# Merge-gate tiles of the second hybrid layer and value tiles of the spatial mixer: two matmuls a block with halves added by VectorE, in place of three

## The reference

```python
def hybrid_layer(x, y, ...):            # called for layer 0 and layer 1
    hx = rms_norm(x, norm_w) * (1.0 + scale_x) + shift_x
    rq, rk, rv, rg, nq, nk, nv, ng, gq, gk, gv, gg, mg = split_cols(hx @ w_in)
...
def merge_branches(ret_o, na_o, gqa_o, gate_logits, w_ret_o, w_na_o, w_gqa_o, w_out):
    g_ret, g_na, g_gqa = jnp.split(jax.nn.sigmoid(gate_logits), 3, axis=-1)
    m = g_ret * (ret_o @ w_ret_o) + g_na * (na_o @ w_na_o) + g_gqa * (gqa_o @ w_gqa_o)
    return m @ w_out
...
def spatial_gating_mixer(x, w_in, v_norm, w_s, b_s, w_out):
    u, v = jnp.split(jax.nn.gelu(x @ w_in), 2, axis=-1)
    v = rms_norm_2(v, v_norm)
```

## Time and profile before

| | |
|---|---|
| median of 3 runs | 1982.38 us (1981.38 to 1985.36) |
| the profiled execution | 1981.85 us, of which the span in the trace is 1980.1 us |
| TensorE busy | 1952.4 us, 99% of the span, 13237 matmuls |
| VectorE busy | 1217.8 us, 62% |
| ScalarE busy | 891.7 us, 45% |
| mean granted clock of TensorE | 0.998 |

### The profile page before, as it was taken

How to read it: one execution, slowest core, us unless ns; L and a number is a source line. 1 busy time by engine, 2 the same in 40 slices (tenths; PEclk the granted TensorE clock), 3 DMA queues, 4 the chain that set the end, 5 groups by cost and what they waited for, 6 DMA issues and landing times. The chain is left out here.

```text
span 1980.1 us, 35364 instructions
## 1 busy us (share of the span) xinstructions
PE 1952.4 (99%) x13237; PEld 1705.6 (86%) x13237; DVE 1217.8 (62%) x1965; ACT 891.7 (45%) x1422; POOL 218.0 (11%) x230
## 2 busy tenths in 40 slices
PE   8999999999999999999999999999999999999998
PEld 6777887777787788998998999989998999999997
DVE  6554443355443655546567777887678677677675
ACT  5444232244432544335554445764445444554443
POOL 1000100111122101211111000000001000201000
PEclk9999999999999999999999999999999999999999
DMA  8221443411234323343355554445555555445553
GB/s 324 78 73 66 147 145 129 142 62 57 82 104 159 105 94 106 108 139 118 128 171 182 188 182 167 155 158 190 181 185 198 181 186 185 160 150 181 181 187 109
DMA packets 79429, 289.23 MB, mean 146 GB/s; under 512 B 8912, under 2 KB 9168, under 8 KB 79312
## 3 DMA queue, kind: packets, MB, share of 16 engines
q1 hardware_dynamic: 77616, 281.61, 42.2%
q0 software_dynamic: 1120, 4.72, 0.8%
q10 hardware_dynamic: 576, 1.24, 0.2%
HBM read 286.49 MB, written 1.05 MB: 145 GB/s over the span
## 5 line engine op out<-in xcount | busy, mean ns | idle before, releaser
L1947 DVE TENSOR_TENSOR w_lo<-raw,w_hi 128x1024 fp32r<-128x1024 f32 x484 | 597.8, 1240 | 306.5 <-ACT w_hi L1643 305.7
L1643 ACT ACTIVATE w_hi<-raw 128x1024 fp32r<-128x1024 f32 x484 | 507.5, 1055 | 405.5 <-PE bank L2562 249.6
L2568 PE MATMUL bank<-h,w_hi 128*128 128x512 f32 x1376 | 491.1, 399 | 1.3 <-DVE h L2069 0.8
L2560 PE MATMUL bank<-h,w_hi 128*128 128x512 f32 (+1 forms) x1344 | 473.2, 352 | 3.6 <-issue 1.7
L2561 PE MATMUL bank<-h,w_hi 128*128 128x512 f32 (+1 forms) x1344 | 452.9, 337 | 0.0
L2562 PE MATMUL bank<-h,w_lo 128*128 128x512 f32 (+1 forms) x1344 | 452.4, 337 | 0.0
L2570 PE MATMUL bank<-h,w_lo 128*128 128x256 f32 x1376 | 386.3, 281 | 0.0
L2568 PEld LDWEIGHTS bank<-h,w_hi 128*128 128x128 f32 x1376 | 258.7, 188 | 62.0 <-DVE h L2069 1.4
L2560 PEld LDWEIGHTS bank<-h,w_hi 128*128 128x128 f32 x1344 | 254.5, 189 | 54.1 <-issue 28.2
L2562 PEld LDWEIGHTS bank<-h,w_lo 128*128 128x128 f32 x1344 | 254.6, 189 | 27.9
L2561 PEld LDWEIGHTS bank<-h,w_hi 128*128 128x128 f32 x1344 | 255.1, 190 | 24.2 <-issue 1.9
(11 more groups left out here) (257 smaller groups left out, 2366.1 us busy)
## 6 DMA issues: line engine op xcount, KB each, us to landing
raw<-in_weights SPq DMA_DIRECT2D x516, 512.0 KB, 3.3
early<-in_first SPq DMA_DIRECT2D x10, 512.0 KB, 13.4
bias<-in_rpb POOLq DMA_DIRECT2D x8, 384.0 KB, 3.4
early_o<-in_first SPq DMA_DIRECT2D x4, 512.0 KB, 16.3
x<-in_tokens SPq DMA_DIRECT2D x2, 512.0 KB, 6.0
x<-in_tokens ACTq DMA_DIRECT2D x2, 512.0 KB, 8.6
work<-in_first SPq DMA_DIRECT2D x2, 512.0 KB, 16.6
out<-cols_out SPq DMA_DIRECT2D x4, 256.0 KB, 2.5
```

The costliest lines, as they stand in the source:

```text
L1643: nc.scalar.activation(w_hi[:, n % SPLIT, :], raw[:, t % RAW, :], ACT.Copy).then_inc(hi_ready, 1)
L1947: dve.tensor_tensor(w_lo[:, t % RAW, :], raw[:, t % RAW, :], w_hi[:, SPLIT_NO[t] % SPLIT, :].bitcast(F32), ALU.subtract).then_inc(lo_ready, 1)
L2560: nc.tensor.matmul(dst, w_hi[:, SPLIT_NO[t] % SPLIT, at], hi, start=start, stop=False, skip_group_check=shared)
L2568: nc.tensor.matmul(bank[:, :], w_hi[:, SPLIT_NO[t] % SPLIT, at], h[:, k, 0:BOTH], start=k == 0, stop=k == KC - 1, skip_group_check=True)
```

## The change

The 24 gate tiles of layer 1 (in layer 0 they stay) and the value tiles 2 to 7 of the spatial mixer (0 and 1 are in a pair product and stay) take the form of the feed-forward: per block one 512-column matmul with w_hi and one 256-column matmul with w_lo. For the gate tiles hi and lo lie 512 columns apart in h, so the 512 columns are two pieces of 256 (h_wide).

For the gate tiles VectorE gets a new step, merge_gate: it adds the bank's halves into merge_tanh and frees the bank. ScalarE's tanh then works in place on merge_tanh, waits for that sum (through g_free), and counts mg_ready, for which VectorE's merge_step waits. For the value tiles VectorE adds the halves into sg_v, waits for its own sum, and multiplies by the root in a second instruction, which frees the bank.

```diff
@@ -431,8 +431,8 @@
 
         return dict(src="h", norm=first.pop("h", None))
 
-    def proj(what, n):
-        return s.product(what, n=n, **src())
+    def proj(what, n, how=None):
+        return s.product(what, n=n, how=how, **src())
 
     def key(name, g, job=None):
         g.k_job = s_add_evac(job or proj(name, BOTH), "key", g)
@@ -606,8 +606,9 @@
         br = ("na", "ret", "gqa").index(branch)
         mg = []
         for dc in (2 * q, 2 * q + 1):
-            job = proj("mg", live)
-            mg.append(s.add_after_split("merge_gate", job=job, slot=dc % 2, before=merged["mg"][dc % 2], cols=live))
+            job = proj("mg", live, how="halves" if layer else None)
+            mg.append(s.add_after_split("merge_gate", job=job, slot=dc % 2, before=merged["mg"][dc % 2], cols=live,
+                                        at=s.count("mg_halves") if layer else None))
             if branch == "na":
                 ada_tiles()
         if branch == "gqa":
@@ -1048,7 +1049,7 @@
 
     s.later(2, first_v)
     for n in range(2, KC):
-        job = s.product("sg_v", n=SEQ, src="h", norm=None)
+        job = s.product("sg_v", n=SEQ, src="h", norm=None, how="halves")
         s.add("sg_v", job=job, c=n, norm=norm)
         up = s.add_after_split("sg_gelu", c=n)
         square(s, vnorm, n, 1, up, after_split=True)
@@ -1125,6 +1126,7 @@
         h = sb("h", [P, KC, 2 * BOTH], F32R)
         h_hi, h_lo = h[:, :, 0:BOTH], h[:, :, BOTH:]
         h_low = h[:, :, SEQ:BOTH]
+        h_wide = h[:, :, :].rearrange("p k (b t) -> p k b t", b=2)
         par = sb("par", [P, NPARAM])
         con = sb("con", [P, NCONST])
         c_silu = sb("c_silu", [P, KC, 32])
@@ -1713,6 +1717,11 @@
 
             def merge_gate_step(st):
 
+                if st.at is not None:
+                    act.wait_ge(*evacuated(st.job))
+                    v = merge_tanh[:, st.slot, 0:st.cols]
+                    nc.scalar.activation(v, v, ACT.Tanh, scale=0.5).then_inc(mg_ready, 1)
+                    return
                 act.wait_ge(*complete(st.job))
                 if st.before is not None:
                     act.wait_ge(*evacuated(st.before.job))
@@ -2084,7 +2093,14 @@
 
             def sg_v_step(st):
 
-                scaled_product(st, sg_v[:, st.c, :], st.norm)
+                if st.job.how is None:
+                    scaled_product(st, sg_v[:, st.c, :], st.norm)
+                    return
+                v = sg_v[:, st.c, :]
+                dve.wait_ge(*complete(st.job))
+                dve.tensor_reduce(v, halves_added(bank_of(st.job)), AX_X, ALU.add).then_inc(halves_summed, 1)
+                dve.wait_ge(halves_summed, st.c - 1)
+                dve.tensor_tensor(v, v, rstd[:, 0:SEQ], ALU.mult).then_inc(evacuated(st.job)[0], 1)
 
             def sg_u_step(st):
 
@@ -2152,6 +2168,20 @@
                                          scalar=1.0, in1=G[st.job.n % 2][:, 0:st.cols], op0=ALU.add, op1=ALU.mult)\
                     .then_inc(g_free[st.job.n % 2], 1)
 
+            def halves_added(bank):
+
+                return bank[:, :].rearrange("p (b t) -> p t b", b=2)
+
+            def merge_gate_step(st):
+
+                if st.at is None:
+                    return
+                dve.wait_ge(*complete(st.job))
+                if st.before is not None:
+                    dve.wait_ge(*evacuated(st.before.job))
+                dve.tensor_reduce(merge_tanh[:, st.slot, 0:SEQ], halves_added(G[st.job.n % 2]), AX_X, ALU.add)\
+                    .then_inc(g_free[st.job.n % 2], 1)
+
             th_count = [0]
             turned = [None, None]
 
@@ -2159,7 +2189,10 @@
 
                 c = st.cols
                 dve.wait_ge(*complete(st.job))
-                dve.wait_ge(*evacuated(st.gate.job))
+                if st.gate.at is None:
+                    dve.wait_ge(*evacuated(st.gate.job))
+                else:
+                    dve.wait_ge(mg_ready, st.gate.at + 1)
                 if st.br and st.add_n >= 2:
 
                     dve.wait_ge(added, st.add_n - 1)
@@ -2561,11 +2594,11 @@
                 nc.tensor.matmul(dst, w_hi[:, SPLIT_NO[t] % SPLIT, at], lo, start=False, stop=False, skip_group_check=shared)
                 return nc.tensor.matmul(dst, w_lo[:, t % RAW, at], hi, start=False, stop=stop, skip_group_check=shared)
 
-            def halves(bank, w, k):
+            def halves(bank, w, k, both):
 
                 t, blk = w
                 at = slice(P * blk, P * blk + P)
-                nc.tensor.matmul(bank[:, :], w_hi[:, SPLIT_NO[t] % SPLIT, at], h[:, k, 0:BOTH], start=k == 0,
+                nc.tensor.matmul(bank[:, :], w_hi[:, SPLIT_NO[t] % SPLIT, at], both, start=k == 0,
                                  stop=k == KC - 1, skip_group_check=True)
                 return nc.tensor.matmul(bank[:, 0:SEQ], w_lo[:, t % RAW, at], h_hi[:, k, 0:SEQ], start=False,
                                         stop=k == KC - 1, skip_group_check=True)
@@ -2587,6 +2620,10 @@
                     if job.src == "h":
                         if job.norm:
                             pe.wait_ge(h_lo_ready, job.norm.chunks[i].h + 1)
+                        if job.how == "halves":
+                            both = h[:, i, 0:BOTH] if job.what in MIXER_TILES else h_wide[:, i, :, 0:SEQ]
+                            ins = halves(bank_of(job), (job.tile, i), i, both)
+                            continue
                         hi = h_hi[:, i, 0:n]
                         lo = h_low[:, i, :] if job.what in MIXER_TILES else h_lo[:, i, 0:n]
                     elif job.src == "m":
```

More of the change, by code:

```diff
@@ L1290, in block_kernel @@
         th_ready = sem("th_ready")
+        mg_ready = sem("mg_ready")
+        halves_summed = sem("halves_summed")
         head_copied = sem("head_copied")
@@ L2538, in _ @@
                    "split_x": split_x_step, "rec_y": rec_y_step, "sg_v": sg_v_step, "sg_u": sg_u_step,
-                   "bank_residual": bank_residual_step, "gate": gate_step, "merge": merge_step, "gated_residual": gated_residual_step,
+                   "bank_residual": bank_residual_step, "gate": gate_step, "merge_gate": merge_gate_step, "merge": merge_step, "gated_residual": gated_residual_step,
                    "fold_weights": fold_weights_step,
@@ L2883, in up @@
                         else:
-                            ins = halves(bank, (t, k), k)
+                            ins = halves(bank, (t, k), k, h[:, k, 0:BOTH])
                     ins.then_inc(tile_used, 1)
```

## The result

The changed kernel took 2009.60 us (median of 4 runs, 2008.06 to 2009.77) against 1981.88 us for the kernel before in the same runs (1981.36 to 1985.36): ratio 1.0132, 95% interval 1.0119 to 1.0144, 1.3% slower. The prediction was 2008.0 us, 1999 to 2014. The profiled execution has a span of 2006.3 us, against 1980.1.

A forecast was written before the change was run, and what follows sets the result against it. TensorE, busy 99% of the span, was taken to bound the kernel. Merge losses of 26.3 us less 0.3 us from the value tiles gave 26.0 us more than 1981.85 or 1982.38 us: 2008 us, range 1999 to 2014.

The forecast's parts named there:

- Tile saves 0.05 us: Each changed gate or value tile on TensorE takes 2.83 us instead of 2.88, 1.5 us in all.
- First half stands 0.49, second 1.75: In a layer 1 merge, TensorE's two output-product halves wait 0.49 and 1.75 us for VectorE's sums; merge 10.93 against 8.96.
- rival 1: Layer 1 merges: tanh does not hold the next w_hi; merge 10.49 us, kernel 2000 us; chance 0.12.
- 7 pattern merges and the first NA merge: Three NA and four GQA merges lose 1.97 us each, 13.8 us; the first NA merge loses 1.5.
- RET merges 11.0 us: Layer 1's four RET merges: second and third lose 6.5 us together, the fourth 2.5, the first 2.0.
- the pattern's 2.0 us: The ordinary merge's loss of 1.97 us, taken as 2.0 for the first RET merge as the nearest.
- Sum 26.0 us: Whole kernel: 26.3 us lost in layer 1's merges less 0.3 us gained in the value tiles.
- Rival 3: TensorE's clock falls in layer 1's merges, half their products at 1.2 GHz adding 51 us: 2059 us; chance 0.03.
- rival 2: Layer 1 merges: sums free the banks in time; 5 us gained, 1977 us, or 1981 with old stalls; chance 0.05 together.

The follow-up runs named there:

- experiment 1: The changed kernel with VectorE's sum of a gate tile's halves moved ahead of the next weight split: 1985.43 us, ratio 1.0008 to the kernel before.
- experiment 5: The changed kernel with three matmuls a block in gate tiles, VectorE copying the bank behind w_lo: 2004.27 us, ratio 1.0105 to the kernel before.
- Experiment 3: The changed kernel with both tanh of a merge after the w_hi behind the second gate tile: 2004.01 us, ratio 1.0104 to the kernel before.
- experiment 7: The changed kernel with the new gate-tile form only in layer 1's four RET merges, value tiles changed: 1993.89 us, ratio 1.0057 to the kernel before.
- 4: The kernel before with ScalarE's tanh of a gate tile ahead of the next w_hi in layer 1: 1984.38 us, ratio 1.0008.
- 6: The kernel before with value tiles in the new form, their sum behind the next weight split: 1992.36 us, ratio 1.0044.
- 9: The changed kernel, sums ahead of the split, output tile's split behind its first half's merge step, GQA m_hi and m_lo a separate step: 1984.49 us, ratio 1.0006.
- 11: The kernel before with NA merges 2 to 4 and GQA merges reordered, three matmuls throughout, tanh ahead of the next w_hi: 1981.00 us, ratio 0.9990.

## Why the prediction was right

The cause, the sum behind w_lo, is shown by 1 and 5: moved ahead of the split, the loss of 1.3% falls to 0.08% (interval -0.01 to 0.17%); and gate tiles with three matmuls lose 1.05% once VectorE takes the bank behind w_lo.

- *Tile saves 0.05 us.* 2.83 us for the gate tile with its two separate pieces, as in the FFN. The value tiles gave 0.5 us instead of 0.3: there a tile went from 2.88 to 2.77 us, twice the FFN's gain, and no run shows why.
- *First half stands 0.49, second 1.75.* They start 3.28 and 6.58 us after the boundary, worked out as 3.32 and 6.59. Merge 10.91 us, predicted 10.93. Experiment 3 shows the tanh's part in it: without it a merge is 10.43, the 10.49 of rival 1.
- *7 pattern merges and the first NA merge, 15.3 us.* Measured 7.4 + 7.6 = 15.0.
- *RET merges 11.0 us.* Measured 10.3 in the trace and 10.2 alone: from the second merge's first half product to the third's it is 25.82 us (945.01 to 970.83) against 22.71 (933.62 to 956.33), 3.1 where 3.27 was worked out; the first and the fourth have the other 4.1, where 4.5 was. The fourth came as worked out (waits of 0.45 and 2.23 us for 0.5 and 2.0). The first was given the pattern's 2.0 us for want of a row, and that it came near is luck: its first half does not wait at all, its second waits for 0.81 us, and TensorE waits for 1.24 us, where it was 0.53, for ScalarE's copies ahead of the product with the values.
- *Sum 26.0 us.* The stretch gave 25.3, the value tiles -0.5: 24.8. The profiled executions are 26.2 apart: this one was already 1.0 us later at the start of the stretch, and about 0.4 us came where its clock fell at 1321 us (26.22 us apart before it, 26.59 behind it). The medians are 27.7 apart, with the interval 23.6 to 28.5.
- *Rival 3.* The clock did not fall at the 24 waits of this execution; at the eight of experiment 7 it fell once, and once at those of experiment 5, for 1.5 us each (last section). The Trainium skill (TensorE: Matmul & The Clock Gate, "A second HAM failure mode: psum-queue depth-cycling") lets such waits swing the gate; as a standing effect no run here shows it, since 24 waits in 200 us left the merges' windows at 1.00.

One sentence of the prediction was wrong: that without w_lo ahead the kernel would gain 5 us (rival 2). It counted what the waits of the kernel before would give back and did not ask what is late next. The expectation of experiment 1 made the same mistake. Experiments 1 and 4 showed it: the merge step, at w_hi + w_lo behind the boundary, frees the next gate tile's bank 0.1 us before it is wanted (868.99 + 0.42 + 0.15 = 869.56 against 869.69). Rival 2's condition, met in experiment 1, gives 1985 us and not 1977.

## What to carry to other kernels

When the engine that frees a bank is changed, work out its place in the new engine's queue, and what that queue waits for, before the price of the instruction: here 0.05 us a tile was bought with 1 us. If the evacuation has to move, put it ahead of the next weight split, as in experiment 1 and in the value tiles. And a wait of TensorE is worth only the distance to the wait behind it: all handovers of the cycle (bank, product, bank) have to be worked out before a gain is booked.

## What I had not expected of the hardware

TensorE's granted clock falls for a few us in most of the profiled executions. The falls that bear on this case come behind a wait of TensorE, but not every wait brings one. All thirteen have one wait of 2.34 or 2.35 us at the same place, ahead of the first product with mix_hi (1294.55 us in the kernel before, 1320.77 in the changed one). In seven of them the granted clock fell to 0.50 within 2 us of its end: in the changed kernel and in experiments 1, 4, 6, 7, 9 and 11. In the other six, the kernel before among them, it stayed at 1.00.

Among the merges it fell in none of the changed kernel's 24 waits, and in one place of experiments 5 and 7 each. In experiment 7 (windows: us, busy time and count by engine, then the granted clock, the DMA share and GB/s):

```profile
984.00:985.00 1.00, 1.00 (x8) 0.67 (x5) 0.41 (x1) 0.00 (x0) 0.00 (x0) 0.50 0.00 0
...
987.00:990.00 3.00, 3.00 (x28) 3.00 (x27) 1.98 (x3) 1.36 (x2) 0.74 (x1) 1.00 0.49 173
```

0.50 is the level of 1.2 GHz, 1.00 that of 2.4. There TensorE had stood for 2.24 us before 982.87, and then 16 matmuls took 1.61 us and 12 took 2.48, where the same ones in the changed kernel's trace, after a wait of 2.23 us, took 1.02 and 1.53 at a clock of 1.00. That is 1.5 us. In experiment 5, after a wait of 1.97 us before 987.48, they took 1.90 and 2.20 us, again 1.5 to 1.6 us more. So a wait of this length can be followed by the lower level and need not be.

This can be part of why executions of one kernel differ by a few us. Of the 66 executions of the kernel before that ran beside the experiments, the 38 with a mean granted clock of 0.995 or 0.996 took 1984.2 us in the median and the 28 with 0.997 or 0.998 took 1982.3. That is a correlation; no run changes the clock alone.
